# Mixture-of-experts tail: sixteen light units alone at the end instead of twelve, and two light units between the last split-form expert's turning and its next down unit

## The reference

```python
def swiglu(x, w1, w3, w2):
    return (jax.nn.silu(x @ w1) * (x @ w3)) @ w2

def moe(hn, w_router, w1, w3, w2):
    ...
    top_v, top_i = lax.top_k(logits, TOP_K)
    top_w = jax.nn.softmax(top_v, axis=-1)
    combine = jnp.sum(jax.nn.one_hot(top_i, N_EXPERTS, dtype=jnp.float32) * top_w[..., None], axis=1)
    out = jnp.zeros_like(t)
    for e in range(N_EXPERTS):
        out = out + combine[:, e:e + 1].astype(t.dtype) * swiglu(t, w1[e], w3[e], w2[e])
    return out.reshape(B, S, D)
```

## Time and profile before

| What | Value |
|---|---|
| Runs, median of 3 | 1207.67 us |
| Profiled execution, own time | 1206.29 us |
| Its span, first to last instruction | 1204.6 us |
| TensorE busy with matmuls | 1189.1 us (99%) |
| VectorE busy | 741.1 us (62%) |
| ScalarE busy | 593.6 us (49%) |
| DMA, mean over the span | 319 GB/s, 384.82 MB |
| DMA in the second half | 425 to 429 GB/s in every full slice |

### The profile page before, as it was taken

One profiled execution on the slowest core, in us unless ns is written; L12 is line 12 of the kernel. 1 busy time (PEld: TensorE's weight loads), 2 busy tenths in 40 slices (PEclk: granted clock), 3 DMA queues, 4 the chain that ended last, 5 costly groups with the idle time before them and its releaser, 6 DMA issues.

```text
span 1204.6 us, 15901 instructions
## 1 busy us (share of the span) xinstructions
PE 1189.1 (99%) x6454; PEld 916.8 (76%) x6454; DVE 741.1 (62%) x765; ACT 593.6 (49%) x641; POOL 68.0 (6%) x55
## 2 busy tenths in 40 slices
PE   9999999999999999999999999999999999999997
PEld 8878888888888888888777766777667777577764
DVE  6867765656545857767757565665646665564633
ACT  7667445434336467445554454453535444453420
POOL 0600001000000600000000000000000000000001
PEclk9999999999999999999999999999999999999999
DMA  9753557655555453378999999999999999999997
GB/s 378 310 185 130 177 177 286 217 176 178 205 180 186 159 208 113 111 277 340 384 427 425 427 426 427 427 429 427 426 427 428 427 427 428 426 428 428 427 425 292
DMA packets 36590, 384.82 MB, mean 319 GB/s; under 512 B 4337, under 2 KB 4337, under 8 KB 7985
## 3 DMA queue, kind: packets, MB, share of 16 engines
q1 hardware_dynamic: 34672, 374.83, 77.2%
q0 software_dynamic: 1696, 8.66, 2.0%
q10 hardware_dynamic: 144, 0.26, 0.1%
HBM read 379.80 MB, written 7.61 MB: 322 GB/s over the span
## 4 chain that ended last, share of the span: by engine, by line
PE 86%; DMA 6%; issue 3%; DVE 3%; POOL 1%; ACT 1%; SPq 0%; POOLq 0%; DVEq 0%; ACTq 0%
PE ps L639 21%; PE ps L641 21%; PE ps L640 21%; PE ps L1737 16%; DMA raw<-in_pairs 4%; PE ps L1263 3%; DVE wl L634 1%; DMA h<-in_x 1%; DMA back<-y_rows,yidx 1%; PE ps L1625 1%; POOL rst L777 1%; PE ps L1637 1%; PE ps L1322 1%; ACT wh L616 0%; DVE h L2441 0%
## 5 line engine op out<-in xcount | busy, mean ns | idle before, releaser
L634 DVE TENSOR_TENSOR wl<-raw,wh 128x2048 fp32r<-128x2048 f32 x152 | 350.5, 2309 | 200.0 <-ACT wh L616 199.6
L616 ACT ACTIVATE wh<-raw 128x2048 fp32r<-128x2048 f32 x152 | 291.1, 1918 | 211.1 <-PE ps L641 167.5
L639 PE MATMUL ps<-wh,XT 128*128 128x512 f32 x856 | 340.1, 397 | 0.3 <-DVE wl L634 0.3
L641 PE MATMUL ps<-wh,XT 128*128 128x512 f32 x856 | 333.9, 390 | 0.0
L640 PE MATMUL ps<-wl,XT 128*128 128x512 f32 x856 | 333.4, 389 | 0.0
L634 DVE TENSOR_TENSOR wl<-ring,wh 128x2048 fp32r<-128x2048 f32 x66 | 151.0, 2291 | 89.8 <-ACT wh L616 89.2
L639 PEld LDWEIGHTS ps<-wh,XT 128*128 128x128 f32 x856 | 160.7, 188 | 40.3 <-issue 8.1
L641 PEld LDWEIGHTS ps<-wh,XT 128*128 128x128 f32 x856 | 160.6, 188 | 34.3
L640 PEld LDWEIGHTS ps<-wl,XT 128*128 128x128 f32 x856 | 160.9, 188 | 31.5
L616 ACT ACTIVATE wh<-ring 128x2048 fp32r<-128x2048 f32 x66 | 126.4, 1915 | 95.4 <-PE ps L641 70.1
L1737 PE MATMUL ps<-ring,few_X 128*64 128x256 f32 x704 | 80.6, 381 | 1.5 <-DMA ring<-in_pairs 1.5
(11 more groups left out here) (294 smaller groups left out, 1149.1 us busy)
## 6 DMA issues: line engine op xcount, KB each, us to landing
raw<-in_pairs SPq DMA_DIRECT2D x65, 2048.0 KB, 17.6
ring<-in_pairs SPq DMA_DIRECT2D x63, 2048.0 KB, 17.6
raw<-in_units SPq DMA_DIRECT2D x86, 1024.0 KB, 5.0
ring<-in_lasts SPq DMA_DIRECT2D x4, 1024.0 KB, 15.6
raw<-in_lasts SPq DMA_DIRECT2D x4, 1024.0 KB, 17.2
y_rows<-in_zeros POOLq DMA_DIRECT2D x7, 512.0 KB, 7.9
raw<-in_boot SPq DMA_DIRECT2D x5, 512.0 KB, 7.6
y_rows<-ys POOLq DMA_DIRECT2D x4, 512.0 KB, 10.6
```

The lines of the kernel that those rows point to most:

```text
L616: nc.scalar.activation(wh[:, U.split_slot(j), :], U.raw(j), ACT.Copy).then_inc(hi_ready, 1)
L634: nc.vector.tensor_tensor(wl[:, s, :], U.raw(j), wh[:, s, :].bitcast(F32), ALU.subtract).then_inc(lo_ready, 1)
L639: nc.tensor.matmul(o, xh, bh, start=start, stop=False)
L641: return nc.tensor.matmul(o, xl, bh, start=False, stop=stop)
```

## The change

It has two parts. The constant FEW_ALONE goes from 12 to 16: the rate at which light units become due falls a little, and the last stretch alone is four units longer. And the function `with_turning_covered` takes the two light units that stand last before expert 5's unit 30 and puts them right behind it, in the order of use alone; the order of loads stays as `moe_orders` makes it.

```diff
-FEW_FROM, FEW_ALONE = 6, 12
+FEW_FROM, FEW_ALONE = 6, 16
...
+def with_turning_covered(units):
+
+    first = (CHAIN[-1], 2 * SLICES + 2 * WIDE - 2)
+    few = [unit for unit in units[:units.index(first)] if unit[0] in SMALL][-2:]
+    rest = [unit for unit in units if unit not in few]
+    at = rest.index(first) + 1
+    return rest[:at] + few + rest[at:]
+
+
 LOADS, TAKEN = moe_orders()
-LOADED, IN_USE = units_in(LOADS), units_in(TAKEN)
+LOADED, IN_USE = units_in(LOADS), with_turning_covered(units_in(TAKEN))
```

## The result

The changed kernel takes 1210.34 us (median; 1208.57 to 1212.18), the kernel before 1207.84 us beside it (1206.91 to 1209.86). The ratio is 1.0021, with a 95% interval of 1.0015 to 1.0028: it is slower by 2.5 us. The forecast was 1208.1 us with a range up to 1210.2, and no change that can be measured was the likeliest outcome.

What follows compares the result with a forecast made beforehand. The DMA engines were taken to set the pace to the end. Last load at 1195.5 plus 1.83, 0.5, 0.1 and 2.73 gave 1200.7 against 1200.31; +0.4 on 1207.67 made 1208.1 us, range 1205.3 to 1210.2.

Steps and rivals of the forecast that it cites:

- The DMA engines never run dry: From about half the span: 2.4, later 4.6 loads of 4.9 us are in flight, so the engines stay full.
- The last load: At the end: the last weight load lands at 1195.5 instead of 1193.1, 2.4 us later.
- the gathers: In the tail: issued near 1171, about 9 us earlier, they move bytes before the last weights have landed.
- The new wait: Before expert 5's unit 30: TensorE waits 3.4 us and loses up to 1.7 us more at the lower clock.
- The turning: At expert 5's transposes, 1157.71 to 1160.24: covering 2.1 us idle and 1.7 us of low clock takes off 3.8 us.
- The fourth case: Wait before unit 30 holds the ring and delays a load: 5.1 us if it reaches the DMA engines, 1212.8 us; chance 0.06.

Runs made afterwards that it cites:

- cover_only: The kernel before (twelve light units alone) with only light units 16 and 17 moved behind expert 5's unit 30; 1208.49 us, ratio 1.0006.
- stall_only: The kernel before with only expert 2's light units 20 to 23 loaded behind expert 0's unit 32 and used just ahead of it; 1208.97 us.
- mid_fixed: The changed kernel with expert 2's light units 20 to 23 loaded and used around expert 0's end as in the kernel before; 1208.73 us, ratio 1.0007.
- gathers_late: The changed kernel with the four gathers held until TensorE has used light unit 24 of the last expert; 1210.20 us, ratio 1.0018.
- mid_gathers: mid_fixed with the four gathers held until TensorE has used light unit 24 of the last expert; 1207.82 us, ratio 1.0002.
- in_step: mid_gathers with the light pair used behind unit 30 loaded behind the pair that holds unit 30, not ahead; 1208.08 us, ratio 1.0003.
- alone16_only: The kernel before with sixteen light units alone and no units moved behind unit 30; 1211.10 us, ratio 1.0026.
- in_step_12: cover_only with the light pair used behind unit 30 loaded behind the pair that holds unit 30; 1208.06 us, ratio 1.0002.

## Why the prediction was wrong, step by step

**The DMA engines never run dry.** This is the step that failed. I took it from the median issue to landing, 12.0 us in 600:650, and held it against the 4.9 us of one load at full rate. Two things were wrong. The stretch I should have asked for was where the order changed: the table changes all along, and I priced only its end. And the bound was too low: engines fall idle while a load is still in flight, and not only when the last one has landed. In cover_only nothing is issued from 1147.0 to 1166.0, and the loads in flight land at 1164.1 and 1168.9:

```profile
1162.00:1164.00 2.00, 2.00 (x19) 1.31 (x20) 0.42 (x1) 0.38 (x1) 0.00 (x0) 0.91 0.71 303
1164.00:1166.00 2.00, 2.00 (x21) 1.16 (x17) 0.00 (x0) 0.00 (x0) 0.00 (x0) 1.00 0.59 254
```

With two loads left the share is 0.71, with one 0.59. In 690:696 of the changed kernel, where a load was issued with only one other in flight (it landed near 693.3), issue to landing of 8.9 to 10.6 us was already too little. The missing term was +1.4 us (stall_only) to +1.6 us (mid_fixed against the changed kernel).

**The forecast without that step.** mid_fixed is the change as I had priced it. It takes 1208.73 us with an interval from 0.9998 to 1.0016, 0.9 us over before; forecast was +0.4. The difference is within what is measured, so the runs neither contradict the rest of the sum nor confirm it.

**The last load.** Forecast 1195.5, of which 2.4 us for the gathers. It landed at 1197.92. stall_only's lands 2.45 us later than before's, 1.5 us of it by missing weights. Holding the gathers back brings the load forward by 2.2 (gathers_late) and 2.8 us (mid_gathers against mid_fixed), near the 2.4 us of the forecast. For the time it is worth at most 0.9 us by the medians, as the path goes over to the gathered rows. The gathers began at 1175.20 and not near 1171: expert 5 ended 2.8 us later than forecast, and the write ahead of them took 12.2 us to the first gather and not 11.3.

**The new wait.** Forecast 3.4 us and up to 1.7 us of clock; measured 4.0 us and (1 - 0.91) x 20 = 1.8 us in 1140:1160. That it stands beside the path fits in_step, which has neither and is no faster. Expert 5 ended at 1161.6 against 1158.8, 2.6 us of it from its load's landing at 1143.1 where I had 1140.5.

**The turning.** The 2.1 us went, and were worth nothing by themselves: with twelve alone +0.0006, with sixteen 1211.10 goes to 1210.34, intervals overlapping.

**The fourth case.** I gave it 0.06 because queues of 22.7 us should stand a stall of 5.1. The stall of the issues was 18 us, as SyncE's loads stand in one order behind a buffer that was held to 1155.8. So it reached the DMA engines' mean, 394 GB/s, as the case had it; but its price of 5.1 us was not paid: alone16_only has neither this stall nor the wait (427 GB/s in 1140:1160) and is no faster than the changed kernel, and in_step without them is no faster than mid_gathers.

**The clock.** The three last units of the profiled execution took 7.09 us and not 5.46. No term had this. It may stand in the median too: of the 20 executions, the 14 with a mean granted clock of 0.995 or 0.996, the profiled one among them, have a median of 1210.9 us, and the six with 0.997 or 0.998 one of 1209.3. The mean is over the whole execution, so this is a hint and not shown. stall_only's profiled execution is at its median, with three last units of 5.62 us, so its 1.4 us hold no such part.

## What to carry to other kernels

Where a table or a planner sets the order, go through the whole order of loads and of uses before pricing the place that the change is about, and ask for every load whether its buffer now comes free later. Such a place cost 1.4 us here where issue to landing was about 10 us; the other places that changed between 720 and 1140 left the rate at 427 GB/s (mid_fixed, with a median of 17.3 us). Hold issue to landing against about two loads' time and not one; no sharp limit is shown, as 600:650 before has a shortest of 9.5 us and runs at 425 GB/s. And where the DMA engines are full, a wait that is covered on TensorE can come back as a wait for data, as in in_step: ask first when the last load lands.

## What the runs showed that I had not expected

- Busy tenths of nine hide a loss of several per cent; the GB/s line showed it (416 and 408 among 426 to 429).
- An idle time of nearly the same length in front of the last units left TensorE at a granted clock of 1.00 in three kernels (2.38 us, three units in 5.62 us in stall_only and 5.68 us in mid_fixed; 2.52 us and 5.64 us in in_step_12) and took it down in two others (2.48 us in the changed kernel, 0.52 in 1195:1198, and 2.51 us in in_step, 0.57 in 1192:1195; 7.09 us each). In alone16_only a shorter one, 2.13 us, took it to 0.50 in 1190:1192, and a pair took 5.36 us and not 3.67. So the length alone does not decide it.

```profile
1188.69 5.36 PE L1737 MATMUL ps<-ring,few_gT 128*64 128x256 f32 x32 [2.13 <-DMA ring<-in_pairs]
```

- The mean rate of the 16 engines from 1180 to the last load's landing is 353 to 371 GB/s in five kernels whose loads were issued without a long gap (335 in alone16_only), and 395 to 419 in seven with a gap of over 13 us.
